# Six delta rule jobs made tokens by channel in 512 columns and turned by VectorE through DRAM

## What is computed

```python
p = rms_norm(h, norm_g) @ w_in                       # even layer
qkv = silu(causal_depthwise_conv(qkv_a, conv_qkv))   # 4 taps over tokens, per channel
q, k, v = heads(qkv); q = l2_norm(q) * DK ** -0.5; k = l2_norm(k)
o = gated_delta_rule(q, k, v, beta, g)               # 8 heads of 128
o_a = rms_norm(o, dn_norm_g) * silu(z_a)
# beside it: a GLU with a 31-tap conv and layer norm, and attention into 256 memory tokens
h = h + concat([o_a, o_b, o_m]) @ w_out
# odd layer: stick-breaking attention (16 heads) and the memory attention, then w_out
```

## Time and profile before

| | |
|---|---|
| median of 3 runs | 1327.3 us (1326.93 to 1327.31) |
| profiled execution | 1326.4 us |
| its span | 1324.7 us |
| busy share of the span | PE 99%, PEld 85%, DVE 74%, ACT 56%, POOL 8% |
| granted TensorE clock | full in all 40 slices |
| transfers | 258 MB, 195 GB/s, queue q1 busy in 61% of 16 engines' span |

### The profile page before, as it was taken

The page is one execution under the profiler, slowest core; times in us unless marked ns, Lnnn a source line. Parts: engine busy times, 40 slices in busy tenths (PEclk is TensorE's granted clock), DMA queues, the critical chain, the costliest instruction groups (busy, mean ns, idle before and its releaser), DMA issues.

```text
span 1324.7 us, 18077 instructions
## 1 busy us (share of the span) xinstructions
PE 1318.0 (99%) x6685; PEld 1120.9 (85%) x6685; DVE 985.3 (74%) x1518; ACT 745.8 (56%) x1167; POOL 104.4 (8%) x103
## 2 busy tenths in 40 slices
PE   9999999999999999999999999999999999999998
PEld 9998899888888888888888888888888888888887
DVE  5557589898998998686656477797788788666563
ACT  6546633476435555576346456747757558554341
POOL 1000301003010100000000020020110200000000
PEclk9999999999999999999999999999999999999999
DMA  9655464455756995665455755765775766964662
GB/s 312 199 176 183 145 195 140 149 174 159 231 170 203 298 287 189 214 203 182 151 180 147 249 174 164 236 190 165 232 205 161 238 191 189 282 213 143 206 191 80
DMA packets 154672, 258.18 MB, mean 195 GB/s; under 512 B 24368, under 2 KB 38617, under 8 KB 154585
## 3 DMA queue, kind: packets, MB, share of 16 engines
q1 hardware_dynamic: 151865, 252.32, 61.2%
q10 hardware_dynamic: 2720, 4.72, 1.1%
HBM read 243.76 MB, written 13.24 MB: 194 GB/s over the span
## 4 chain that ended last, share of the span: by engine, by line
PE 79%; DVE 1%; POOL 0%; issue 0%; DVEq 0%
PE job L1846 48%; PE job L1856 24%; PE mixer L1867 1%; PE mixer L2059 1%; PE mixer L2079 1%; PE mixer L2088 1%; PE mixer L2096 1%; PE mixer L1976 0%; PE mixer L2087 0%; PE mixer L2098 0%; PE mixer L1956 0%; DVE cvr L1611 0%; DVE wlo L1363 0%; PE mixer L1989 0%; PE mixer L1964 0%
## 5 line engine op out<-in xcount | busy, mean ns | idle before, releaser
L1846 PE MATMUL job<-whi,xhi 128*128 128x512 f32 x1532 | 610.9, 399 | 0.0
L1846 PE MATMUL job<-whi,xlo 128*128 128x512 f32 x1532 | 597.4, 390 | 0.0
L1363 DVE TENSOR_TENSOR wlo<-raw,whi 128x1024 fp32r<-128x1024 f32 x431 | 529.0, 1247 | 77.2 <-ACT whi L1015 76.3
L1015 ACT ACTIVATE whi<-raw 128x1024 fp32r<-128x1024 f32 x431 | 444.7, 1055 | 198.5 <-PE job L1856 145.2
L1856 PE MATMUL job<-wlo,xhi 128*128 128x512 f32 x1532 | 409.9, 389 | 0.0
L1856 PEld LDWEIGHTS job<-wlo,xhi 128*128 128x128 f32 x1532 | 287.6, 188 | 60.6
L1846 PEld LDWEIGHTS job<-whi,xlo 128*128 128x128 f32 x1532 | 288.0, 188 | 57.4
L1846 PEld LDWEIGHTS job<-whi,xhi 128*128 128x128 f32 x1532 | 287.8, 188 | 57.6
L1611 DVE SCALAR_TENSOR_TENSOR cvr<-cvr,vt 128x255 f32<-128x255 f32 (+14 forms) x240 | 106.4, 500 | 0.2
L1843 PE MATMUL job<-xhi,whi 128*128 128x256 f32 x376 | 94.1, 288 | 0.0
L1843 PE MATMUL job<-xlo,whi 128*128 128x256 f32 x376 | 92.1, 283 | 0.0
(11 more groups left out here) (297 smaller groups left out, 973.0 us busy)
## 6 DMA issues: line engine op xcount, KB each, us to landing
raw<-in_od_w_in_dram SPq DMA_DIRECT2D x160, 512.0 KB, 4.4
raw<-in_ev_w_in_dram SPq DMA_DIRECT2D x143, 512.0 KB, 4.1
raw<-in_ev_w_out_dram SPq DMA_DIRECT2D x48, 512.0 KB, 5.5
raw<-in_od_w_out_dram SPq DMA_DIRECT2D x48, 512.0 KB, 5.4
raw<-in_w_mem_kv_dram SPq DMA_DIRECT2D x32, 512.0 KB, 4.7
proj<-turned_blocks SPq DMA_DIRECT2D x48, 128.0 KB, 4.6
turned_blocks<-proj SPq DMA_DIRECT2D x8, 512.0 KB, 4.7
turned_weights<-mix SPq DMA_DIRECT2D x16, 192.0 KB, 4.6
```

The lines of the kernel that those rows point to most:

```text
L1015: act(whi[:, c % RING, :, :], raw[:, c % RAWS, :, :], ACT.Copy).then_inc(s_hi, 1)
L1363: vec.tensor_tensor(wlo[:, c % RING, :, :], raw[:, c % RAWS, :, :], whi[:, c % RING, :, :].bitcast(F32), ALU.subtract).then_inc(s_lo, 1)
L1846: mm(pj[j % 2][n][:, :], x[:, s, cols], h, start=first, stop=False)
```

## The change

The six channel jobs become token jobs (`CHANNEL` is empty), so ScalarE copies them out, and the turned rstd row goes. Then three new steps for each bring q, k and v into the layout that the delta rule reads. `nt` (VectorE) turns the 32 x 32 blocks of a job, in two instructions of 128 x 512, into a stage buffer. `nw` (SyncE) writes that to DRAM with four DMAs in pieces of 32 elements (128 B). `nr` (SyncE) reads it back into the job's slot with four DMAs of 4 KB a partition, which gives channels on partitions and tokens along. The first tap of a group waits for the last read. The delta rule starts four chunks later in both groups, the GLU of group 0 four chunks later too (that of group 1 at the same place), the copy of job 4 as well, and the taps of the long convolution move with them. `do_open` is rewritten for the token form. Three semaphores of the stick-breaking heads become one, with threefold counts, in the same order of steps.

```diff
@@ -81,7 +81,8 @@
 _jobs()
 J_ZB, J_QM, J_ZM, J_OA, J_MEM, J_OB, J_OM, J_ODIN, J_ODOUT = 12, 14, 16, 18, 22, 26, 30, 34, 54
 ADDED = [j for j in range(len(JOBS)) if JOBS[j][0] in ("ev_out", "od_out")]
-CHANNEL = [0, 1, 2, 6, 7, 8]
+CHANNEL = []
+QK_TURNED = [0, 1, 2, 6, 7, 8]
 COPIED = [j for j in range(len(JOBS)) if j not in ADDED and j not in CHANNEL]
 CH0 = []
 _n = 0
@@ -137,7 +138,7 @@
 
 
 VECTOR_SHARE = {"evac": .5, "dnC": 1.3, "dnU": .5, "dnV": .35, "dnR": .25, "dnG": .4, "inF": 2.7, "inT": .55, "d4y": .4, "d5c": .15,
-                "d5e": .1, "d6": .25, "gate": .25, "za": .45, "glu": .45, "zg": .65, "lt": .47, "xt": .18, "mf": .16, "bas": .1}
+                "d5e": .1, "d6": .25, "gate": .25, "za": .45, "glu": .45, "zg": .65, "lt": .47, "nt": .5, "xt": .18, "mf": .16, "bas": .1}
 TENSOR_SHARE = {"dnB": .26, "dnG": .55, "d4x": .32, "d4y": .45, "d5a": .08, "d5b": .16, "d5c": .16, "d5d": .08,
                 "d5e": .08, "d7": .08, "gT": .08, "xt": .08}
 
@@ -212,14 +213,14 @@
     for n in range(4, KT):
         stream(0, n // 2 - 1, [(("xt", n), 0)])
     stream(0, 6, [(("vec", 0), 0)])
-    stream(0, 6, [(("rstd", 0), 3), (("rrow", 0), 0)])
+    stream(0, 6, [(("rstd", 0), 0)])
     stream(0, RING + 1, [(("baw", 0), 1), (("ba", 0), 2), (("bat", 0), 4), (("bas", 0), 0)])
 
     work, last = deltanet(0)
-    p = stream(1, after(J_V[0]), work)
+    p = stream(1, after(J_V[0]) + 4, work)
     stream(1, p, last)
     work, last = deltanet(1)
-    start = max(int(p) + 3, after(J_V[1]))
+    start = max(int(p) + 3, after(J_V[1]) + 4)
     p = stream(1, start, work)
     for g in range(2):
         stream(1, after(J_ZA[g]) - 1, [(("za", g), 0)])
@@ -239,7 +240,10 @@
         stream(5, CH0[J_ODOUT + 8] + k // 2 - 1, [(("mf", F_ODD + 16 + k), 0)])
 
     for g in range(2):
-        stream(2, after(J_GLU[g] + 1) + 6 * g, [(("glu", g), 2 + g)] + [(("gT", ct), 1) for ct in range(4 * g, 4 * g + 4)])
+        stream(2, after(J_GLU[g] + 1) + 4 + 2 * g, [(("glu", g), 2 + g)] + [(("gT", ct), 1) for ct in range(4 * g, 4 * g + 4)])
+
+    for j in QK_TURNED:
+        stream(3, CH0[j + 1] + (4 if j == 0 else 1), [(("nt", j), .5), (("nw", j), 2.5), (("nr", j), 0)])
 
     def turn_job(e, start, back=2):
 
@@ -255,19 +259,19 @@
     for e in (4, 5):
         q = stream(3, max(turn_job(e, max(after(TURNED[e]) - 1, int(oa))) + 3, q), [(("zg", e), 1)])
     for j in range(len(JOBS)):
-        late = 5 if j == J_GLU[1] + 1 else 0 if J_OM <= j < J_ODIN or j == len(JOBS) - 1 else 1 if j else 3
+        late = 5 if j in (J_GLU[0] + 1, J_GLU[1] + 1) else 0 if J_OM <= j < J_ODIN or j == len(JOBS) - 1 else 1 if j else 3
         stream(-1, CH0[j + 1] + late, [(("evac", j), 0)])
     vector, tensor = [0.47] * NCH, [1.0] * NCH
     for pos, _, _, step in placed:
         if 0 <= pos < NCH:
             vector[pos] += VECTOR_SHARE.get(step[0], 0) if step[0] != "evac" or step[1] not in COPIED else 0
             tensor[pos] += TENSOR_SHARE.get(step[0], 0)
-    left, behind, p = list(range(4 * TAPS)), 0.0, after(J_GLU[0] + 1) + 3
+    left, behind, p = list(range(4 * TAPS)), 0.0, after(J_GLU[0] + 1) + 7
     while left:
         behind = max(-0.7, behind + vector[p] - tensor[p])
         while left and behind + CONV_SHARE <= CONV_ROOM:
             pr, d = divmod(left[0], TAPS)
-            if p < after(J_GLU[pr // 2] + 1) + 7 * (pr // 2) + 4 + 2 * (pr % 2):
+            if p < after(J_GLU[pr // 2] + 1) + 3 * (pr // 2) + 8 + 2 * (pr % 2):
                 break
             stream(2, p, [(("conv", left.pop(0)), 0)])
             if d == TAPS - 1:
@@ -452,6 +456,7 @@
 
 
         dram_w = nc.dram_tensor("turned_weights", (2, 128, 384), F32, kind="Internal")
+        dram_n = nc.dram_tensor("turned_qk", (32, 4, 4, T, 4, 32), F32, kind="Internal")
         dram_x = nc.dram_tensor("turned_blocks", (len(TURNED), 128, 1024), F32, kind="Internal")
 
         def slot(a):
@@ -464,17 +469,25 @@
         tanhs = {0: slot(2), 1: slot(3), 4: tiles(20), 5: tiles(0), 10: slot(0), 11: slot(1)}
 
         turn_no = {i: n for n, i in enumerate(i for st, i in plan if st == "lt")}
+        turn_count = {q: n + 1 for n, q in enumerate(q for q in plan if q[0] in ("lt", "nt"))}
 
         def exchanged(e, transfers=5):
 
             return s_xg[turn_no[e] % 3], 80 * (turn_no[e] // 3) + 16 * transfers
 
         def blocks_turned(e):
-            return s_jt, turn_no[e] + 1
+            return s_jt, turn_count["lt", e]
 
         def weights_exchanged(h, transfers=5):
 
             return s_sx[h % 2], 80 * (h // 2) + 16 * transfers
+
+        def qk_stage(j):
+            return tiles(16) if j < 6 else slot(PSLOT[J_ZA[0]])
+
+        def qk_exchanged(j, transfers=8):
+
+            return s_nx, 128 * QK_TURNED.index(j) + 16 * transfers
 
         def landed(e):
             return slot(PSLOT[TURNED[e]])
...
@@ -693,6 +705,8 @@
             if J_QM <= j < J_ZM:
                 return [(s_glu, 2), (s_za, 2), (s_z, 4 * (j - J_QM) + 4)]
             for g in range(2):
+                if q == J_ZA[0]:
+                    return [(s_za, 1), qk_exchanged(8, 4)]
                 if q == J_GLU[g]:
                     return [(s_gtp, 4 * g + 4)]
                 if q == J_GLU[g] + 1:
@@ -831,6 +845,20 @@
                     sp.wait_ge(s_t[1], LEVELS + 1)
                 sp.dma_start(tinv8, rows_t).then_inc(s_inD, 16)
 
+            def do_nw(j):
+                sp.wait_ge(s_jt, turn_count["nt", j])
+                if j:
+                    sp.wait_ge(*qk_exchanged(j, 0))
+                for a in range(4):
+                    sp.dma_start(bass.AP(dram_n, 32 * a, [[4096, 32], [128, 32], [1, 32]]),
+                                 qk_stage(j)[32 * a:32 * a + 32].rearrange("p (m j) -> p m j", j=32)).then_inc(s_nx, 16)
+
+            def do_nr(j):
+                sp.wait_ge(*qk_exchanged(j, 4))
+                for b in range(4):
+                    sp.dma_start(slot(PSLOT[j])[32 * b:32 * b + 32], bass.AP(dram_n, 1024 * b, [[4096, 32], [1, 1024]])
+                                 ).then_inc(s_nx, 16)
+
             def do_xw(e):
                 sp.wait_ge(*blocks_turned(e))
                 if turn_no[e] >= 3:
...
@@ -1112,6 +1140,7 @@
 
             def do_dnC(h):
                 sc.wait_ge(*evac_done(J_V[h // 4]))
+                sc.wait_ge(*qk_exchanged(J_V[h // 4]))
                 if h >= 4:
                     sc.wait_ge(s_5cp, h - 3)
                 for c in range(3):
...
@@ -1680,6 +1709,16 @@
                 vec.scalar_tensor_tensor(out=v, in0=M[3][:, S:2 * S], scalar=1.0, in1=v, op0=ALU.add, op1=ALU.mult
                                          ).then_inc(s_z, 1)
 
+            def do_nt(j):
+                ve.wait_ge(*evac_done(j))
+                if j in (1, 2, 7, 8):
+                    ve.wait_ge(*qk_exchanged(j - 1, 4))
+                elif j == 6:
+                    ve.wait_ge(s_za, 1)
+                for t in range(T):
+                    ins = vec.transpose(qk_stage(j).rearrange("p (b h t j) -> p t h b j", b=4, h=4, t=T)[:, t], proj[:, PSLOT[j], t, :])
+                ins.then_inc(s_jt, 1)
+
             def do_lt(e):
                 j = TURNED[e]
                 ve.wait_ge(*evac_done(j))
...
@@ -1816,10 +1855,10 @@
                         pe.wait_ge(s_xh, k + 1)
                         if k == 1:
                             pe.wait_ge(s_hi0, 2)
-                    for n in range(4):
+                    for t in range(T):
                         a, b = (xlo if i == 1 else xhi), (wlo if i == 2 else whi)
-                        ins = mm(pj[0][n // 2][:, S * (n % 2):S * (n % 2) + S], b[:, 0, k, 128 * n:128 * n + 128],
-                                 a[:, SLOT[k], :], start=(i == 0 and k == 0 and n % 2 == 0), stop=False, skip_group_check=True)
+                        ins = mm(pj[0][t][:, :], a[:, SLOT[k], 128 * t:128 * t + 128], b[:, 0, k, :], start=(i == 0 and k == 0),
+                                 stop=False)
                 if i == 2:
                     ins.then_inc(s_pe, 1)
 
```

More of the change, by code:

```diff
@@ L595, in prog @@
         s_xg = [sem(f"turned_blocks_exchanged{i}") for i in range(3)]
+        s_nx = sem("qk_exchanged")
         s_zp = sem("gates_transposed")
@@ L622, in prog @@
         s_sbA = sem("sb_log_terms")
-        s_sbsp = sem("sb_softplus")
         s_sbk = sem("sb_masks_made")
-        s_sbcs = sem("sb_sums_scanned")
-        s_sbar = sem("sb_log_weights")
+        s_sbar = sem("sb_softplus_then_sums_then_log_weights")
         s_sbE = sem("sb_exponentials")
@@ L677, in read @@
                     "mas": (s_exp, i + 1), "mat": (s_pt, i + 1),
-                    "mao": (s_mao, i + 1), "sbT": (s_sbT, i + 1), "sbz": (s_sbar, i + 1),
+                    "mao": (s_mao, i + 1), "sbT": (s_sbT, i + 1), "sbz": (s_sbar, 3 * i + 3),
                     "sbo": (s_sbo, i + 1)}[step]
@@ L860, in do_sr @@
                                  bass.AP(dram_w, 49152 * (h % 2) + 96 * b, [[384, 32], [12288, 4], [1, 96]])).then_inc(s_sx[h % 2], 16)
```

(16 more changed lines are left out.)

## The result

The change makes the kernel slower, by 0.3%: 1331.2 us as a median of 8 runs (1327.61 to 1336.28), against 1326.95 us of the kernel before in the same rounds (8 runs, 1326.18 to 1327.38). The ratio is 1.0034, with an interval of 1.0024 to 1.0045. The forecast was 1320.8 us. The spread is news by itself: 8.7 us, where before has 1.2. The profiled execution of after is the slowest of its runs, 1336.28 us, with a span of 1334.5.

What follows compares the result with a forecast made beforehand. TensorE, busy 99% of the span, was taken to bound the kernel. Savings of 0.3 us in the first chunks and 6.2 later, all else 0, made 6.5 us: span 1318.2, median 1320.8 us, range 1318.3 to 1325.5.

Steps and rivals of the forecast that it cites:

- The delta rule, GLU and taps four chunks later: Moving these blocks in the plan was to lose 0 to 2 us, taken as 0.
- the sign I gave: The forecast is wrong if TensorE's waits outside the head grow by more than 2 us.
- The places I did look at: VectorE's weight remainders after the small inversions, now before chunks 58 and 109: ready 1.1 and 0.7 us ahead of TensorE.
- rival (b): VectorE becomes late after the inversions or in the updates, 1 to 2 us back at each place: 1322.5 to 1326 us; 14%.
- The updates of group 0 at the faster pace: Group 0's inversion updates at 2.72 us a chunk, where group 1's had waited 0.5 us: cost taken as 0.
- The pace: New token chunks take 2.72 us, not the channel chunks' 2.88: 0.16 us less each.
- the middle: Chunks 9 to 23 and 48 to 71, 39 in all, save 0.16 us each: 6.2 us.
- The head: First chunks, up to the small product's wait before chunk 9: 0.3 us saved, bounds 0 and 2.0.
- The exchange: q, k and v through DRAM: reads land 13 to 20 us after TensorE ends the V job, hidden, 0 us.
- Rival (c): The exchange lands late, its writes taking 31 us, so TensorE stands 18 and 13 us: 1352 us; 10%.
- The evacuations: Copying jobs out moves to ScalarE, 8 us more there, VectorE unchanged: 0 in time, hidden under TensorE.
- The sum: 6.5 us saved in all, 0.3 in the first chunks and 6.2 later: a median of 1320.8 us.

Runs made afterwards that it cites:

- e5: The kernel before, channel jobs kept, with only the plan's shift of delta rule, GLU, copy and taps four chunks later: 1337.87 us, ratio 1.0083.
- e7: The changed kernel with the plan of before and without the exchange of q, k and v, so the token form alone: 1323.38 us, ratio 0.9975.
- e9: The kernel before, channel jobs kept, with the shift of four chunks and both transfer moves of e4: 1327.64 us, ratio 1.0007.
- e4: The changed kernel with the first turned job's exchange three chunks later and the reads of turned jobs 2 and 3 four chunks later: 1321.99 us, ratio 0.9962.
- e1: The changed kernel run again, unchanged, for a second profile: 1330.61 us, ratio 1.0028.
- e12: e4 with the small product of the beta and decay columns one chunk later: 1320.90 us, ratio 0.9955.
- e13: e4 without the exchange of q, k and v, dropped after planning so every other step keeps its place: 1322.56 us, ratio 0.9964.
- e2: The changed kernel with only the exchange of the first turned job three chunks later: 1329.54 us, ratio 1.0014.
- e8: The changed kernel with group 1 of the delta rule three chunks earlier, one later than in the kernel before; group 0 stays: 1325.35 us, ratio 0.9992.
- e11: The changed kernel with only ScalarE's gate step of turned job 4 three chunks later, reads still bunched: 1324.99 us, ratio 0.9987.
- e3: The changed kernel with only the reads of turned jobs 2 and 3 four chunks later, behind those of job 4: 1323.54 us, ratio 0.9974.
- e10: e4 with the exchange of q, k and v left out before planning, so the taps of the long convolution were placed differently: 1325.88 us.

## Why the prediction was wrong

**The step that failed** is "The delta rule, GLU and taps four chunks later", taken at 0 of 0 to 2 us. Its cost was 11 us by itself (e5), 10.2 of it in two orders of transfers; in after the two orders cost 9.2 us (1331.20 - 1321.99). I had looked for what VectorE has queued behind the inversions, and at what ends the even layer. I hadn't walked SyncE's queue at the new positions: which transfers were tied to the delta rule and moved, which were tied to their own job and didn't, and what that did to their order. Both facts stand in the plan and could have been worked out: the load of group 1's inverses moved from position 104 to 108, past the write of the first turned job at 107, and the reads of turned jobs 2 and 3 from 136 and 137 to 140 and 141, where those of job 4 stand at 141. What the trace of before didn't hold was the half clock behind each idle time, 3.4 us at A and 2.8 at B in the profiled execution. By the sign I gave, the forecast is wrong if TensorE's waits outside the head grow by more than 2 us; they grew by 7.2 (0.5 before; 4.8, 2.1 and 0.8 after).

**The places I did look at held, and were never as tight as I had them.** The remainder for chunk 58 was there at 186.23 + 1.2 = 187.4 us, and TensorE began the chunk at 188.47: 1.0 us, forecast 1.1. That for chunk 109 at 354.02 + 1.2 = 355.2, the chunk at 356.34: 1.1 us, forecast 0.7. But I had counted to the wrong moment. TensorE waits for a chunk's remainder (`s_lo`) only in front of the last third of its matmuls, 1.8 us into a token chunk:

```profile
186.23 3.48 DVE L1392 TENSOR_TENSOR wlo<-raw,whi 128x1024 fp32r<-128x1024 f32 x3
```
```profile
190.29 1.07 PE L1895 MATMUL job<-wlo,xhi 128*128 128x512 f32 x4
```

So the cover was 2.8 us at chunk 58 (190.29 - 187.4) and 2.9 at chunk 109 (358.15 - 355.2), and the 14% for rival (b) rested in part on a danger that wasn't there. VectorE late at these two places didn't happen. The updates of group 0 at the faster pace, taken at 0, waited in no kernel with the whole change; in e7 they did, for 1.8 us.

**The pace held, the middle was somewhat too high.** Between e9 and e4, which differ by the token form and exchange alone, chunks 9 to 23 gain 2.2 us of the 15 x 0.16 = 2.4 forecast. Chunks 48 to 71 gain 3.0 of 3.8: 0.14 us each up to chunk 55 and 0.12 behind, where the steps of the delta rule lie between the matmuls. Why there it is less stays open. From chunk 111 on 0.4 us more come.

**The head** was taken at +0.3 us. e9 to e4 shows -0.4 at chunk 9; in after it was -1.5, as ScalarE waited 1.75 us for a weight chunk at 29.55 us and the small product began at 40.31, not near 38.5 (38.61 in e1, which had no such wait):

```profile
40.31 0.32 PE L1944 MATMUL mixer<-xhi,whi 128*48 128x256 f32 x1 [1.86 <-DVE whi L1455]
```

In the kernel before chunk 9 started at 42.6 us; in the kernels with the new head (all but e5, e9 and e12) it lies between 42.0 and 45.3, and after alone has 44.1 in one execution and 42.4 in the other (e1). So the head varies from one execution to the next by more than the term. That the wait of the small product keeps the gain was right: taken away, it gives 1.1 us.

**The exchange held.** The first reads were issued at 94.44 us. TensorE had begun chunk 24 at 86.2, and the first tap ran at 102.15, so the reads were in at T + 16, forecast T + 13 to T + 20:

```profile
102.15 1.31 ACT L1148 ACTIVATE reg<-proj,vt 128x256 f32<-128x256 f32 x3 [1.02 <-DMA proj<-turned_qk]
```

The tap waited 1.0 us for them, forecast none, and nobody behind it was late. The writes of 128 B pieces landed 3.0 us after issue (2.5 taken), the reads 5.5 (4.6 taken). Rival (c) didn't happen: e13 shows no cost of the exchange. Its price was also too high as I worked it out. A write has 1024 pieces and the 7.7 us load 2048, so four writes as dear by the piece take 4 x 3.85 = 15.4 us, not 31 (which is 4 x 7.7), and the reads would be in at about T + 25: 3 us late, not 18.

**The evacuations** are hidden, as taken: ScalarE's busy time rose by 5.7 us (745.8 to 751.5), VectorE's stayed at 985.3.

**The sum** was 6.5 us; the form with the exchange is worth 5.65. With the two orders mended the kernel takes 1321.99 us, and with the small product moved 1320.90. The kernel that the forecast stands for is the first of these, and for it 1320.8 is 1.2 us too low. That e12 meets it within 0.1 us is luck, since the forecast kept the wait of the small product.

## What to carry to other kernels

When a block of steps moves in a plan, list every transfer at its old and new position in the issuing queue: steps that count from the moved block go along, steps that count from something else stay, and where they meet the order turns over or the transfers bunch. Then ask of each late transfer which in-order engine stands in front of it and what else that engine has behind; moving this wait behind the other work gave back 6.2 us here without touching a transfer. And an experiment that leaves work out must keep the place of everything else.

## What the runs showed of the hardware

**A gap of TensorE costs more than itself.** Behind 2.10 us without a matmul in A and 4.83 in B the 512 column matmuls ran 0.43 us apart, for 6.8 and 5.5 us: 1.2 GHz in place of 2.4. The Trainium skill gives this distance for the lower clock (TensorE: Matmul & The Clock Gate, section "Back-to-back issue gap": columns by 1.2 GHz, which for 512 makes 0.427 us as an estimate), and the trace agrees. The length of the gap alone doesn't settle whether the clock falls: behind 3.0 us at L1443 in e2 it didn't, behind 3.0 us at L1906 in e8 it did, behind 2.0 at L2015 in e11 and 1.7 there in e1 it did, behind 1.25 there in e3 and 1.8 at L2010 in e7 it didn't. What decides is open.

**This is also more than half of the spread.** The runs of after have mean granted clocks from 0.999 (1327.61, 1329.12 and 1329.21 us) to 0.995 (1335.73 and 1336.28 us). A mean of 0.995 in a span of 1334 us stands for some 13 us at half clock, so at most 6.7 us, less what falls into a gap; against 0.999 that is some 5 of the 8.7 us, and the rest goes with the length of the gaps. In e2 the fastest run, 1323.54 us, had 1.0 and the slowest, 1332.44, 0.996. e3, e4 and e12, whose runs all have 0.999 or 1.0, vary by 0.3 to 0.5 us. The gap in B isn't needed for it: e8, e10 and e11 have none there, but another with half clock behind it, and their runs vary by 4.3 to 4.9 us with clocks down to 0.997.

**Short VectorE instructions can stretch to the length of GpSimd's.** In e10, 0.19 became 1.22 us beside a GpSimd instruction of 1.27 us; another of 0.18 beside the same kind stayed at 0.18.
